# Branch projections and conv taps in the last two pair turns, modulation spread over the merge, paired small products, and new turn orders

## The reference

```
h = RMSNorm(s) * (1 + scale1) + shift1;  z = h @ W_in
A: bidirectional RWKV-7: token shift of r, k, v; data-dependent decay and rate (two small
   up-projections per direction); kk normalised per head; delta-rule state scan of 16 heads of 64,
   forward and backward; then group norm, bonus, gate, output projection
B: GLU -> depthwise conv of 31 taps (rows of the 64-wide grid in layer 0; columns, 15 taps
   that reach anything, in layer 1) -> LayerNorm -> swish -> projection
C: GELU -> LayerNorm -> chunked spatial gating unit over 128 tokens -> projection
s += gate1 * (sum_i sigmoid(g_i) * branch_i) @ w_merge
s += gate2 * SwiGLU(RMSNorm(s) * (1 + scale2) + shift2)
```

## Time and profile before

| | |
|---|---|
| median of 3 runs | 4474.54 us |
| profiled execution | 4475.39 us |
| its span | 4473.6 us |
| TensorE busy | 4219.4 us, 94% |
| VectorE busy | 1365.3 us, 31% |
| ScalarE busy | 1074.1 us, 24% |
| granted TensorE clock, mean | 0.963 |

### The profile page before, as it was taken

The page is one execution under the profiler, slowest core; times in us unless marked ns, Lnnn a source line. Parts: engine busy times, 40 slices in busy tenths (PEclk is TensorE's granted clock), DMA queues, the critical chain, the costliest instruction groups (busy, mean ns, idle before and its releaser), DMA issues. The chain is left out here.

```text
span 4473.6 us, 108758 instructions
## 1 busy us (share of the span) xinstructions
PE 4219.4 (94%) x51156; PEld 2514.7 (56%) x51156; DVE 1365.3 (31%) x2121; ACT 1074.1 (24%) x1778; POOL 58.1 (1%) x52
## 2 busy tenths in 40 slices
PE   7999999988999999999999989999997899999998
PEld 3566666665555555555555556666666344444443
DVE  1555555554730000100000255555554220010000
ACT  2444444442020000100000244444443120010000
POOL 0000000000000000000000000000000000000000
PEclk8999999988999999999999989999998999999999
DMA  5000000003431111111111200000000532222222
GB/s 187 23 8 23 23 22 23 27 20 125 135 124 52 52 49 52 42 52 52 52 52 52 84 23 8 22 21 22 21 31 13 199 111 76 78 68 75 75 80 75
DMA packets 67388, 260.42 MB, mean 58 GB/s; under 512 B 7680, under 2 KB 9984, under 8 KB 66048
## 3 DMA queue, kind: packets, MB, share of 16 engines
q1 hardware_dynamic: 62208, 219.18, 15.4%
q10 hardware_dynamic: 3456, 29.04, 1.6%
q0 software_dynamic: 1280, 5.24, 0.3%
HBM read 239.80 MB, written 13.63 MB: 57 GB/s over the span
## 5 line engine op out<-in xcount | busy, mean ns | idle before, releaser
L584 PE MATMUL psum<-arena,ring 128*128 128x512 f32 (+1 forms) x4992 | 1805.0, 523 | 29.4 <-ACT arena L1326 22.6
L584 PEld LDWEIGHTS psum<-arena,ring 128*128 128x128 f32 x4992 | 950.5, 191 | 890.0 <-issue 816.0
L879 PE MATMUL psum<-arena 32*32 32x32 f32 (+4 forms) x40512 | 835.0, 212 | 147.0 <-issue 112.0
L879 PEld LDWEIGHTS psum<-arena 32*32 32x32 f32 (+3 forms) x40512 | 753.4, 122 | 336.8 <-issue 269.4
L766 PE MATMUL psum<-arena,ring 128*128 128x512 f32 (+1 forms) x1408 | 554.3, 523 | 2.5 <-ACT arena L1419 1.6
L1254 PE MATMUL psum<-arena,ring 128*128 128x512 f32 (+1 forms) x1440 | 520.2, 521 | 0.0
L1254 PEld LDWEIGHTS psum<-arena,ring 128*128 128x128 f32 x1440 | 273.6, 190 | 242.0 <-issue 229.6
L766 PEld LDWEIGHTS psum<-arena,ring 128*128 128x128 f32 x1408 | 254.2, 194 | 201.6 <-issue 178.3
L2161 DVE TENSOR_TENSOR arena<-psum,arena 128x768 f32<-128x768 f32 (+1 forms) x44 | 36.3, 825 | 718.8 <-PE psum L584 718.8
L2102 DVE TENSOR_TENSOR arena<-psum,arena 128x768 f32<-128x768 f32 (+1 forms) x48 | 39.6, 825 | 617.9 <-PE psum L584 617.9
L1698 ACT ACTIVATE arena<-psum 128x768 f32<-128x768 f32 (+1 forms) x44 | 31.0, 704 | 698.8 <-PE psum L584 698.8
(11 more groups left out here) (131 smaller groups left out, 2464.2 us busy)
## 6 DMA issues: line engine op xcount, KB each, us to landing
ring<-w_stream_in SPq DMA_DIRECT2D x408, 512.0 KB, 3.7
x_spill<-arena ACTq DMA_DIRECT2D x2, 3072.0 KB, 8.7
arena<-ya_spill ACTq DMA_DIRECT2D x2, 3072.0 KB, 10.0
arena<-x_spill ACTq DMA_DIRECT2D x2, 3072.0 KB, 18.5
ring<-w_stream_in ACTq DMA_DIRECT2D x8, 512.0 KB, 6.3
arena<-x_in ACTq DMA_DIRECT2D x1, 3072.0 KB, 14.3
arena<-ups_in SPq DMA_DIRECT2D x16, 192.0 KB, 2.4
ya_spill<-arena POOLq DMA_DIRECT2D x8, 384.0 KB, 6.8
```

Source lines behind the costliest of these rows:

```text
L584: mm = eng.matmul(psum[0:lhs[k].shape[-1], tile, a - off:b - off], lhsT=lhs[k], rhs=rhs[k][:, a:b], start=(k == 0), stop=(k == len(lhs) - ...
L879: return pe.matmul(out, lhsT=lhs, rhs=rhs, start=start, stop=stop, skip_group_check=True)
```

## The change

It does these things:

- Turn 8 takes in four projections of the branch (cb0, ca0, cb1, ca1) in the place of k, r, v, with their sigmoid, product and the conv taps of channel 0; turn 9 the projections su0 to su2 with their GELU, and more taps. `LAST_TURN_TAPS` says how many. Buffers of the branch, the reload and the FFN get other places.
- Modulation items: two after each of the remaining nine projections, six after each LayerNorm sum, two after g00, and in layer 0 one after each of the next sixteen merge steps.
- The matmuls of z stand inside the w blocks, ScalarE copies z behind w, and the blocks run w0, w1, u0, w2, u1, g0, u2. For this the four kr tiles are laid out so that a chunk of both directions is 128 columns side by side, and the last three transposed groups are 4 transposes each instead of 8 matmuls.
- Decay and rate products are issued for both directions at once, into banks 0 and 1.
- The first two projections of `lora` and `ffn` share each arriving tile.
- In the first phase the modulation comes before the norm on ScalarE and VectorE.
- ScalarE's table loads are written out, some ahead of the wait before them.
- All `WEAVE` strings are new, with strings for turn 9.

```
-UP_ORDER = ((0, 0), (1, 1), (1, 0), (0, 1))
+UP_ORDER = ((0, 0), (1, 0), (0, 1), (1, 1))
-LANDS = dict(mean=(1, 1), bonus=(1, 0), lw=(0, 0, 0, 1), la=(1, 1, 0, 0), kkn=(0, 0), ...)
+LANDS = dict(mean=(1, 1), bonus=(1, 0), lw=(0, 1, 0, 1), la=(0, 1, 0, 1), kkn=(0, 0), ...)
-BLOCKS = ["w0", "u0", "w1", "u1", "g0", "w2", "u2", "g1", "g2"]
+BLOCKS = ["w0", "w1", "u0", "w2", "u1", "g0", "u2", "g1", "g2"]
...
+EARLY, GELU_EARLY = ("cb0", "ca0", "cb1", "ca1"), ("su0", "su1", "su2")
+LAST_TURN_TAPS = ((18, 0), (15, 15))
...
+def whole_flow(l):
+    for name in ("cb2", "ca2", "cb3", "su3", "ca3", "sv0", "sv1", "sv2", "sv3"):
+        entry(name, 2)
+    entry("smean")
+    out.append(f"t{mod_thirds(l)[0]}")
+    out.extend(itertools.islice(mods, 6))
+    entry("svar", 6)
...
+    entry("g00", 2)
...
+    for n, name in enumerate(merge):
+        entry(name, 1)
...
+        def project_two(eng, tiles, chunks, rhs, c0, ready):
+            for k in range(KT):
+                eng.wait_ge(*ready(k))
+                for x in range(2):
+                    for a, b in halves(c0, c0):
+                        last[x] = eng.matmul(psum[:, tiles[x], a - c0:b - c0], lhsT=lhs[x][k], ...)
...
+                def early_tiles(n, j, k0, k1):
+                        if k == 0:
+                            hold(j, (eu if n % 2 else eg).at(l, 2 * (n // 2) + j))
+                        mm = pe.matmul(bank(j, z=b - a), lhsT=w[k], rhs=hs[k][:, a:b], ...)
...
+                def gelu_tiles():
+                    pe.wait_ge(*yv.at(KT * (l + 1) - 1))
...
+                def up_tiles(t, name, ev, src, n, reader, i):
+                        for d in DIRS:
+                            hold(d, reader.at(g, 2 * i + d))
+                        for d in DIRS:
+                            pe.matmul(bank(d, z=b - a), lhsT=ups_block(g, n, side(d)), rhs=slot(src)[side(d)][:, a:b],
+                                      start=True, stop=True).then_inc(ev.sem, 1)
...
-                            for d in DIRS:
-                                mm = mm64(bank(b, side(d), n * P, n * P + P), slot(kr(g, d, 0), a, a + C), ident, True, True)
-                            continue
+                            src = arena[:, a:a + P]
                         mm = pe.transpose(bank(b, a=n * P, z=n * P + P), src, ident)
...
+                                if kind == "w":
+                                    for d in DIRS:
+                                        rows = side(1 - d)
+                                        mz = mm64(bank(z_bank(i), side(d), at, at + HD), pcols(d, h, c, 0, C, rows), tok(UV, d, c, rows, a, z), True, True)
...
                         act.activation(wk(i * GRP, b=GRP * P), bank(W_BANK), ACT.Copy, scale=-1.0).then_inc(wst.sem, 1)
                         yield
+                        for d in DIRS:
+                            ins = act.activation(tok(UV, d, i * GRP, side(d), b=GRP * P), bank(b, side(d)), ACT.Copy)
+                        ins.then_inc(zst.sem, 1)
...
+            mod_ready(0)
             normed(0, 0)
-            mod_ready(0)
```

More of the change, by code:

```diff
@@ L223 @@
 MOD_ITEMS = 2 * KT
+EXP, SIGMOID, LOG, GELU, SILU = 0, 2, 5, 11, 18
 NORMS = {("norm1", 0): 0, ("norm2", 0): 1, ("norm1", 1): 2, ("norm2", 1): 3, ("final", 1): 4}
-def branch_flow(l):
[L230 to L259, removed]
@@ new lines, in branch_flow, with merge_flow, merge_steps @@
+def branch_flow(l):
+    flow = whole_flow(l)
+    return flow[:flow.index("g00")]
+def merge_flow(l):
+    flow = whole_flow(l)
+    return flow[flow.index("g00"):]
+def merge_steps(l):
+    return [n for n in merge_flow(l) if n[0] in "gpc"]
+def flow_chunks(l):
+    out = list(EARLY + GELU_EARLY)
+    for n in whole_flow(l):
+        if n[0] in "mg" or n[:2] in ("cb", "ca", "su", "sv", "p0") and n != "svar":
+            out.append(n)
+        elif n[:2] in ("p1", "p2") and f"p2{n[2]}" not in out:
+            out.append(f"p2{n[2]}")
@@ L575, in halves, with project @@
             return [(a, b) for a, b in ((c0, min(cut, T)), (max(cut, c0), T)) if a < b]
-        def project(eng, tile, lhs, rhs, c0, off, ready=None):
+        def project_two(eng, tiles, chunks, rhs, c0, ready):
+            lhs = [chunk_blocks(n) for n in chunks]
+            last = [None, None]
+            for k in range(KT):
+                eng.wait_ge(*ready(k))
+                for x in range(2):
+                    for a, b in halves(c0, c0):
+                        last[x] = eng.matmul(psum[:, tiles[x], a - c0:b - c0], lhsT=lhs[x][k], rhs=rhs[k][:, a:b],
+                                             start=(k == 0), stop=(k == KT - 1), skip_group_check=True)
+            return last
+        def project(eng, tile, lhs, rhs, c0, off):
             mm = None
-            for n, (a, b) in enumerate(halves(c0, off)):
+            for a, b in halves(c0, off):
                 for k in range(len(lhs)):
-                    if n == 0 and ready is not None:
-                        eng.wait_ge(*ready(k))
                     mm = eng.matmul(psum[0:lhs[k].shape[-1], tile, a - off:b - off], lhsT=lhs[k], rhs=rhs[k][:, a:b],
@@ L660, in _ @@
                 B = phases[f"branch{l}"]
[L661 removed]
+                done = {name: early.at(l, 2 * n + 1) for n, name in enumerate(EARLY)}
+                loads(f"branch{l}", B["chunks"], lambda name: done[name] if name in done else B["PE"].at("p10" if name == "p20" else name))
                 for key, names in (("res1", res1_chunks), ("ffn", phases["ffn"]["chunks"]), ("res2", res2_chunks)):
@@ L1158, in branch_phase @@
                 freed.clear()
+                freed[2], freed[1] = (phases[f"branch{l}"]["A"].at(n) for n in ("su2", "su1"))
                 key = f"branch{l}"
```

543 lines of the change are left out of this document (340 added, 203 removed).

## The result

The changed kernel takes 4418.37 us (median of 4 runs, 4417.46 to 4430.22), the kernel before on the same chip 4475.18 (4472.16 to 4481.23): a ratio of 0.9877, 95% interval 0.9858 to 0.9897. It is 57 us faster, where 159 were forecast, and the range from 4245 to 4388 does not hold it. The profiled execution took 4418.09 us, with a span of 4416.3.

A forecast was written before the change was run, and what follows sets the result against it. TensorE, busy 94% of the span, was taken as the bound. Filled turns -73.5, turn 0 +2, last two turns and branch (with merge) -81.2, start -6: -158.7 us from 4475.4, so 4316 for the median, range 4245 to 4388.

The forecast's parts named there:

- Filled turns: Scan turns with projections beside them: less TensorE work, -6.0 us in each of 7 in layer 0, -4.5 in layer 1, -73.5.
- rival B: Filled turns: the chain binds, work leaves but turns stay as long, idle grows by 6 us; 4390; chance 0.13.
- Rival D: Filled turns: new orders also remove half of the idle and cold time, 79 us more; 4237; chance 0.20.
- Last scans: Turn 8, each layer's last scan, takes in branch projections: 111 us in layer 0 (+13), 97 in layer 1 (+1.7).
- Turn 9: Turn behind the last scan takes in su0 to su2: +19.4 us in layer 0, +14.7 in layer 1.
- E: Layer ends give half, as taps delay the last scan or weights come late beside the reload; 4357; chance 0.12.
- Branch before its mean: Branch phase: 16 projections become 9, -84.1 us in layer 0 and -59.4 in layer 1.
- Mean to mixing: Branch mean to mixing: modulation bursts of 8 become 6 in layer 0, -7.1 us; new bursts in layer 1, +2.9.
- Merge of layer 0: Merge: 16 modulation items, one to a step, at 1.0 us instead of 0.5, and a pair: +16.7 us.
- Start: First phase: modulation gain comes before the norm, so the first projection starts near 52.5 us: -6.
- Rival A: Decay and rate pairs: TensorE waits for both sigmoids, four waits a turn over 14 turns; 4540 at 4 us; chance 0.04.
- first two savings: Filled turns: z products inside w blocks, -2.4 us a turn, and kk tiles turned by transposes, 3 x -0.43 = -1.3.

The follow-up runs named there:

- e3: Changed kernel with the 16 z products of each group issued behind the 16 w products instead of between them: 4447.61 us, ratio 0.9934 to the kernel before.
- e5: Changed kernel with other turn orders that put projection steps between groups of small products, same steps: 4311.65 us, ratio 0.9657 to the kernel before.
- e8: Kernel before, its work unchanged, with turn orders that keep small products apart: 4376.48 us, ratio 0.9783 to the kernel before.
- e9: Changed kernel with newly planned spread orders and each decay or rate product waiting for its own bank alone: 4294.80 us, ratio 0.9598 to the kernel before.
- e4: Changed kernel with each decay or rate product waiting for its own bank alone, not for both: 4408.74 us, ratio 0.9847 to the kernel before.
- e1: Changed kernel with 1024 more matmuls of 32, 64 and 128 columns behind TensorE's last product, results unused: 4473.03 us (one run).
- e6: Changed kernel with turn orders planned from measured step durations as if instructions came without limit: 4432.86 us, ratio 0.9910 to the kernel before.
- e7: Changed kernel with layer 0's sixteen merge modulation items two behind a step, from the fourth step on, instead of one: 4416.62 us, ratio 0.9865 to the kernel before.
- e10: The kernel with spread orders and single bank waits (e9), with z products behind the w products again: 4308.16 us, ratio 0.9642 to the kernel before.

## Why the prediction was wrong, point by point

Measured times are those of the profiled executions; they are 57.3 us apart, the forecast says 158.7.

- **Filled turns, the step that failed.** "Sum -6.2 of path in a TensorE-bound turn" was taken as -36 for turns 2 to 7 of layer 0 and -27 for those of layer 1; it was -17.9 and +0.3. The work did leave: busy 34.6 and 23.2 less, although half-level time grew by 27 and 51 us. The single costs were right, too: joint block 1.09 for 1.1, a pair of 64x512 products 1.06, single modulation items 0.98. The joint blocks paid as well: taken apart again they cost 29 us (e3). What failed is that the turn was not bound by TensorE's work alone, and that the new orders were taken to give something or nothing ("can give more"), never to cost. The earlier trace rows showed 16675 records in 689.5 us: 130 packets, one in 5.3 us on the mean, where a bunch uses one up in 1.3; the page had the queue's line, and I passed over it. Every edit in these turns took time out but few or no records: z as many as before, the pairs as many, only the transposes 36 fewer a turn. The records left came faster, and the new orders put them closer: 27 and 23 dense steps within the inverse for 41 and 43. Pauses in the six turns went from 26.0 to 31.0 us and from 33.7 to 57.7. No run has the new work with the old orders, so what the orders cost and what the faster records cost is not separated. That is rival B in its outcome (its 4390 is still 28 below), but not by its mechanism: I named the chain, and it was the supply. Pauses of 2.2 to 2.7 us stood in the trace before.
- **Rival D**, new orders that remove half of idle and cold time (4237), had about the size right of what an order can do (79 us priced; 107 from the changed kernel to e5, 97 in e8), but with the orders given idle and half-level time grew. e5 and e9 are what D describes, at 4312 and 4295.
- **Last scans.** +22.0 for +13 and +12.0 for +1.7. In e5 they are 108.6 and 95.7 against my 111 and 97: the estimate of the work held, and another order takes away the rest. Also corrected: the 98.0 and 95.3 of before I read as a chain; in layer 0 there are 21 packets in 98 us, most under 4.1 us apart, and the two scans have 16 and 18 us of pauses of their 22 and 24 idle: supply is a large part of it.
- **Turn 9.** +23.8 for +19.4, and +14.0 for +14.7. The difference in layer 0 is one wait: VectorE gates the second half of the last pair (L2131) behind seven conv taps, and TensorE stands for 5.5 us. The timeline of VectorE there:

```profile
1072.10 0.69 DVE L2131 TENSOR_TENSOR arena<-arena,psum 128x512 f32<-128x512 f32 x1 [0.42 <-PE psum L869]
1072.71 7.50 DVE L1938 SCALAR_TENSOR_TENSOR arena<-arena,par 128x246 f32<-128x246 f32 x14
1080.12 0.41 DVE L2131 TENSOR_TENSOR arena<-arena,psum 128x256 f32<-128x256 f32 x1
```

  In e5 another order takes turn 9 to 35.8. It is E's mechanism, at an eighth of its price.
- **Branch before its mean.** -82.4 for -84.1 and -56.5 for -59.4: right.
- **Mean to mixing.** -4.1 for -7.1, +9.3 for +2.9: in layer 1 the bursts of six wait for weights three times, at clock 0.86.
- **Merge of layer 0.** +26.6 for +16.7: sixteen single items and a pair are 16.7 as said; of the other 9.9 a wait for weights (below) and 3.4 us at half level behind it are some 6, and 4 stay open. The timeline of TensorE:

```profile
1307.92 1.05 PE L740 MATMUL psum<-ring,arena 128*32 128x512 f32 x4 [3.67 <-DMA ring<-w_stream_in]
```

- **Start.** The first projection starts at 51.99 for 52.5 forecast, 6.6 earlier for 6. Turns 0 and 1 gave 1.2 instead of 5 in layer 0 and 0.8 instead of 3.5 in layer 1. `project_two` and the table loads: 0 as said, within what is left (3.2 us more behind the last mixing product of layer 1, for 1).
- **Rival A** is small: its wait is seen in turn 0, where the forecast had 6.2 us of it and the trace has 4.7 in each layer, and e4 gains nothing clear in the filled turns; the 10 us of e4 are not clear of noise. Also corrected: the rule that the prediction turned against its first two savings bears on the first alone, for the second is transposes on the whole array (128*128 in the earlier trace rows); and it would have left the joint block some gain, since w and z write different banks.

The misses by size: filled turns 45, last scans 19, merge 10, branches and turn 9 18, turns 0 and 1 7, the rest 2; together 101. That e5 lands on 4312, next to my 4316, is chance as far as the turns go: on the kernel before, spread orders alone give 97, which I had priced at nothing, and between kernels with orders spread alike (e8 to e5) the work taken out of the filled turns cost 3 us where the forecast had them give 63. The ends of the two layers, from the last scan on, gave -66 from e8 to e5, against the -81 of the forecast; 10 of the difference lie in the merge.

## What to carry to other kernels

Count instructions beside busy time: where small matmuls dominate, look at the instruction queue's line, divide its packets into the records, and see how close together packets start. If a stretch consumes a packet faster than the next can come, shorter instructions there give nothing (in e1, 32 and 64 columns ran at the same pace); put slow instructions between fast ones, or have fewer instructions. Work taken out elsewhere still pays (e3), as long as the order that follows does not draw the fast instructions together. A plan of orders that knows durations and dependencies but not the supply can be worse than none (e6).

## What was not expected of the hardware

- TensorE gets its instructions in 16 KB packets, 128 matmul records with their loads each, 3.21 us apart at the closest in the twelve traces; with nothing else to wait for, runs of 128 records start 3.47 to 4.29 us apart (e1). Below some 30 ns a record the array waits.
- The clock goes with it: 0.50 through the starved stretch of e1, and in filled turns 113 us at half level in the changed kernel, 24 with the same work spread (e5), none in those of e8 (layer 1 each).
- Four runs of one kernel lie 18 us apart for e7, 16 for e3 and e6, 14 for e5, 6 for e8 and 5 for e9 and e10. That pauses make the difference is not shown: e5 and e9 have about as much of them.
